# Two transformer blocks on one core: other start addresses for the split hidden activations of the six feed-forward layers

## The chip, the cores and the metric

The kernel runs on one core of one Trainium2 chip. The metric is the device time of one launch in microseconds: the median of three runs of the kernel before is 1599.71 us (1599.46 to 1599.98).

## The reference

Two blocks run one after the other on 256 tokens of 1024 features, in float32. Each block surrounds its mixers (three kinds of attention merged by gates in the first; a short convolution and a sparse attention in the second) with SwiGLU feed-forward layers, six of them in all:

```python
D_MODEL = 1024
SEQ = 256
D_FF = 2816

def swiglu(x, w_gate, w_up, w_down):
    return (jax.nn.silu(x @ w_gate) * (x @ w_up)) @ w_down

x = layer_norm(alpha * x + 0.5 * swiglu(x, w_gate[0], w_up[0], w_down[0]), ...)
x = layer_norm(alpha * x + hybrid_mixer(x, ...), ...)
x = layer_norm(alpha * x + 0.5 * swiglu(x, w_gate[1], w_up[1], w_down[1]), ...)
```

The change concerns only the last product of `swiglu`, hidden (256 x 2816) times `w_down` (2816 x 1024).

## The kernel before

Every float32 product is made of three products of the type fp32r. Both operands are split into a rounded high part and the rest as a low part, and high*high, low*high and high*low are added up in PSUM. ACT writes the high part (a copy that rounds), DVE the low part (original minus high part). Weights stream from HBM in slabs of 2048 elements per partition through six slots of `raw`; ACT makes `w_hi` and DVE `w_lo` from each (L729, L1160). Low parts overwrite `raw`.

`PHASES` (L49) gives the order of ten phases: six feed-forward layers (`FFN`), the mixer, the convolution, the keys and values, and the sparse attention. A feed-forward layer uses 33 slabs. The first 22 make the hidden activations, 256 features at a time (`tile(j)`, j = 0 to 10). In most tiles the weights are the stationary operand (`features`, L2089 and L2094), so that the result already has its features on partitions; the first two or three tiles have tokens as stationary operand and are turned by a transpose (`hidden`, L2077). Either way ACT and DVE leave the hidden activations as `hT_hi` and `hT_lo`, 22 chunks of 128 features by 256 tokens, in element order `[P, FC, S]` with `FC` = 22 and `S` = 256: ACT at L1096 and L1115, DVE at L1775 and L1794. In between, `silu` and `h` hold the two halves of a tile.

The last 11 slabs are the down product, done by `project` (L1870s). Here the split hidden activations are the stationary operand, 128 features by 128 tokens per weight load, and 512 columns of a weight slab are the moving operand. Per slab, `part` issues eight matmuls high*high, eight low*high, and eight high*low, in this order:

```python
for c, toks, at, o in each:
    nc.tensor.matmul(o, lhs_hi[:, 2 * d + c, toks], hi[:, c, at], ...)      # L1878
for i, (c, toks, at, o) in enumerate(each):
    nc.tensor.matmul(o, lhs_lo[:, 2 * d + c, toks], hi[:, c, at], ...)      # L1883
for c, toks, at, o in each:
    ins = nc.tensor.matmul(o, lhs_hi[:, 2 * d + c, toks], lo[:, c, at], ...)  # L1887
```

That is 24 matmuls for each of 11 slabs, 264 a layer and 1584 in the six layers. Each has a weight load (LDWEIGHTS) of its own.

Memory is laid out by the order of allocation. `layer_memory` frees what it allocates at once, so that the groups of tensors of different phases lie over each other. With `h_pad` (32 elements, 128 bytes), which nothing reads or writes, `hT_hi` starts at byte 179840 of each partition and `hT_lo` at 202368; both are 128 bytes past a multiple of 512. `silu` and `h` follow at 224896 and 226944, also at 128. `xT`, all slots of `w_hi` and of `w_lo`, and the similar operands `oT_hi` and `yT_hi` with their low parts start at 128 past such a multiple too, and 128 fp32r columns are 512 bytes, so every load of 128 fp32r columns in this kernel starts there. Two other groups of fp32r loads do not. In the compression of keys and values (L2383, L2384, L2389) a load has 80 columns and starts at `windows_of(xc_hi)[:, kv, c, part:part + 80]`, with `XC_ROW` = 96 elements from chunk to chunk and `xc_hi` at 0 past a multiple of 512: for `part` 0 the starts are multiples of 128 bytes, for `part` 1 each is 4 bytes further. In the gate product of the sparse attention (L1845, L1846, L1847) a load of `wg_hi` or `wg_lo` has 48 columns and starts at a multiple of 64 bytes.

Of the kernel before, what the change touches and what calls it, by code (L numbers as in the profile page):

```python
# [5 lines left out]
F32 = mybir.dt.float32  # L6
F32R = mybir.dt.float32r
# [5 lines left out]
P = 128  # L13
D = 1024
KC = D // P
S = 256
# [3 lines left out]
FC = FF // P  # L20
# [37 lines left out]
def two_block_kernel(nc, t, out):  # L58
# [5 lines left out]
    with ExitStack() as ctx:  # L64
# [7 lines left out]
        def layer_memory(tensors):  # L72
            with ExitStack() as own:
                return [own.enter_context(nc.sbuf_tensor(n, s, d)) for n, s, d in tensors]
# [32 lines left out]
        MERGED_FIRST = [(0, 0, bank[6]), (1, 0, bank[7]), (0, 1, bank[0]), (1, 1, bank[1])]  # L107

        qk, v_mix, _, oT_hi, oT_lo, gates, b_gate, prob, probT, far, tmp, o_norm = layer_memory([
            ("qk", [P, 6 * BC, S], F32),  # L110
            ("v_mix", [P, NT, 3 * BW], F32),
            ("o_pad", [P, 96], F32),
            ("oT_hi", [P, BC, S], F32R), ("oT_lo", [P, BC, S], F32R),
            ("gates", [P, NT, D], F32), ("b_gate", [P, 3, D], F32),
            ("prob", [P, 2, BW], F32),
            ("probT", [P, 2, BW], F32),
            ("far", [P, BW], F32),
# [35 lines left out]
        q_n = sel_pT[:].rearrange("p a b c -> p (a b c)")[:, 0:NT * D].rearrange("p (t n c) -> p t n c", t=NT, n=2)  # L153
        gate_rows = sel_add[0:3 * NQ, 0:S]
        cmp_l = sel_add[:].rearrange("p (t h n) -> p t h n", t=NT, h=NQ)
        _, hT_hi, hT_lo, silu, h = layer_memory([
            ("h_pad", [P, 32], F32),
            ("hT_hi", [P, FC, S], F32R), ("hT_lo", [P, FC, S], F32R),
            ("silu", [P, NT, 256], F32), ("h", [P, NT, 256], F32)])
        conv_v, conv_a, conv_c, conv_y, _, yT_hi, yT_lo, conv_b = layer_memory([  # L160
            ("conv_v", [P, KC, S + 2], F32), ("conv_a", [P, KC, S], F32), ("conv_c", [P, 2, 512], F32),
            ("conv_y", [P, 2, 512], F32), ("y_pad", [P, 16], F32), ("yT_hi", [P, KC, S], F32R), ("yT_lo", [P, KC, S], F32R),
# [148 lines left out]
        def tail(n):  # L311
            return TAIL + 1 if has_ln(n) and has_rms(n) else TAIL
# [19 lines left out]
        def token_tiles(n):  # L332
            return 3 if n == 0 or behind_kv(n) else 2
# [4 lines left out]
        def hidden_bank(n, j):  # L338
            return bank[4 + j % 2] if token_tiles(n) == 3 else bank[6 + j]
# [382 lines left out]
        def _(act):  # L722
# [10 lines left out]
            def split_to(k):  # L733

                while highs[0] <= k:
                    split(highs[0])
                    highs[0] += 1
# [25 lines left out]
            def boundary(n):  # L763
                split_to(first_slab[n + 1] + 5 - tail(n))
                if n < last:
                    for tt in range(NT):
                        norm(n, [tt])
                        if tt == 1:
                            split_to(first_slab[n + 1] + 3)
                        evacuate_input(inputs_before(n + 1), TOKENS_FIRST[2 * tt:2 * tt + 2], 2 * tt)  # L770
                        if tt == 0 and has_ln(n):
                            split_to(first_slab[n + 1] + 3)
# [22 lines left out]
            for n, kind in enumerate(phases):  # L795
# [293 lines left out]
                    boundary(n)  # L1089
                if kind == FFN:  # L1090
                    f = ffn_number[n]

                    def hidden(j):

                        act.wait_ge(hT_psum, token_before[n] + j + 1)
                        nc.scalar.activation(hT_hi[:, 2 * j:2 * j + 2, :],  # L1096
                                             hidden_bank(n, j)[:].rearrange("p (c m) -> p c m", c=2),
                                             ACT.Copy).then_inc(hT_high, 1)

                    def feature_tile(j):  # L1100

                        before, done = FT * f + j, joined_before[n] + j - token_tiles(n)
                        split_to(s0 + 2 * j + LEAD)
                        act.wait_ge(slab_used, s0 + 2 * j + 2)
                        act.wait_ge(h_ready, 2 * before)
                        for fb in range(2):
                            nc.scalar.activation(silu[:, fb, :], FEATURES[j % 2][fb][:, S:2 * S], ACT.Copy).then_inc(low_half, 1)  # L1107
                        act.wait_ge(hT_ready, before)
                        for fb in range(2):
                            nc.scalar.activation(h[:, fb, :], FEATURES[j % 2][2 + fb][:, S:2 * S], ACT.Copy).then_inc(low_half, 1)  # L1110
                        split_to(s0 + 2 * j + 1 + LEAD)
                        act.wait_ge(gate_joined, done + 1)
                        nc.scalar.activation(silu[:], silu[:], ACT.Silu).then_inc(silu_ready, 2)  # L1113
                        act.wait_ge(h_ready, 2 * before + 2)
                        nc.scalar.activation(hT_hi[:, 2 * j:2 * j + 2, :], h[:], ACT.Copy).then_inc(hT_high, 1)  # L1115

                    def tile(j):
                        if 0 < j <= token_tiles(n):
                            hidden(j - 1)
                        if j >= token_tiles(n):  # L1120
                            feature_tile(j)
                            return
                        split_to(s0 + 2 * j + LEAD)
                        act.wait_ge(slab_used, s0 + 2 * j + 2)
                        for tt in range(NT):
                            if j > 0:
                                act.wait_ge(h_ready, 2 * FT * f + 2 * j - 1 + tt)
                            nc.scalar.activation(silu[:, tt, :], bank[2 * (j % 2) + tt][:, 0:256],
                                                 ACT.Silu).then_inc(silu_ready, 1)
                        split_to(s0 + 2 * j + 1 + LEAD)  # L1130

                    for j in range(3):
                        tile(j)
                    if n == 0:
                        act.wait_ge(lam_dots, 1)
                        nc.scalar.activation(lam_col[:, 2:4], lam_col[:, 0:2], ACT.Exp).then_inc(lam_exp, 1)
                    for j in range(3, FT):
                        tile(j)
                    for d in range(FC // 2):
                        if d < FC // 2 - tail(n):  # L1140
                            split_to(s0 + 2 * FT + d + LEAD)
                    boundary(n)

        @block.vector
        def _(dve):
# [145 lines left out]
            for n, kind in enumerate(phases):  # L1291
# [477 lines left out]
                    boundary(n, 1.0, s0 + 8)  # L1769
                if kind == FFN:  # L1770
                    f = ffn_number[n]

                    def hidden(j):
                        dve.wait_ge(hT_high, FT * f + j + 1)
                        nc.vector.tensor_tensor(hT_lo[:, 2 * j:2 * j + 2, :],  # L1775
                                                hidden_bank(n, j)[:].rearrange("p (c m) -> p c m", c=2),
                                                hT_hi[:, 2 * j:2 * j + 2, :].bitcast(F32),
                                                ALU.subtract).then_inc(hT_ready, 1)
# [63 lines left out]
        def _(pe):  # L1842
# [216 lines left out]
            for n, kind in enumerate(phases):  # L2059
                s0 = first_slab[n]  # L2060
                if kind == FFN:
                    f = ffn_number[n]

                    def gate_up(j, kh, tiles=range(NT)):
                        ins = token_slab(s0 + 2 * j + kh, kh, 512, slice(0, 512), lambda tt: bank[2 * (j % 2) + tt][:], tiles=tiles)
                        if NT - 1 in tiles:
                            ins.then_inc(slab_used, 1)
# [291 lines left out]
                if kind == KV:  # L2359
# [12 lines left out]
                    for kv in range(2):  # L2372

                        pe.wait_ge(xc_ready, 1 + 4 * (kv + 1))
                        for part in range(2):
# [4 lines left out]
                            for c in range(8):  # L2380
                                chunk = 8 * part + c
                                at = slice(part, part + CMP_ROWS)
# [3 lines left out]
                            for c in range(8):  # L2386
                                chunk = 8 * part + c
                                at = slice(part, part + CMP_ROWS)
# [7 lines left out]
                if kind == NSA:  # L2396
# [141 lines left out]
                    for tt in range(NT):  # L2538
                        unit_gone(tt)
                        for g in range(GROUPS):  # L2540
                            p = cmp_p[:, tt, PER_GROUP * g:PER_GROUP * (g + 1), :].rearrange("p r n -> p (r n)")
# [50 lines left out]
```

## Time and profile before

| | |
|---|---|
| median of three runs | 1599.71 us |
| span of the profiled execution, first to last instruction | 1597.9 us |
| that execution's span to the median of the runs | 1.8 us less |
| TensorE busy (matmul) | 1591.1 us |
| VectorE busy | 1031.5 us |
| ScalarE busy | 801.4 us |
| moved by DMA | 291.21 MB |
| mean granted clock of TensorE | 1.000 |

The device time of a run holds the span and some 1.8 us around it. Busy time of matmuls overlaps, since they are pipelined: one of 512 columns shows about 390 ns while the next starts after some 227 ns. What a matmul costs in a stream is therefore read from the distance between starts, and the timeline, which merges equal instructions that follow each other, gives it: the start of one row to the start of the next, divided by the count.

### The profile page before, as it was taken

The page shows a single profiled execution, that of the slowest core. Times are in us where ns is not written, and L with a number is a line of the kernel's source. Part 1 is how long each engine was busy: PE and PEld are TensorE (multiplying, and loading weights), DVE is VectorE, ACT ScalarE, POOL GpSimd, SP SyncE. Part 2 cuts the span into 40 slices and gives each one's busy share as a digit, 9 for nine tenths or more (in the row PEclk, how much of TensorE's full clock was granted, in tenths as well). Part 3 has the DMA queues.
Part 4 walks back from the last instruction along what each step waited for, and adds up shares of the span by engine and source line. Part 5 has one row for each costly group of instructions (what it writes and reads, how often), then busy time and mean ns, then how long its engine had stood idle before and what let it go on. Part 6 is the DMA issues. An engine that isn't in the chain of part 4 may idle for free.

```text
span 1597.9 us, 21193 instructions
## 1 busy us (share of the span) xinstructions
PE 1591.1 (100%) x8788; PEld 1369.5 (86%) x8788; DVE 1031.5 (65%) x1228; ACT 801.4 (50%) x1092; POOL 35.5 (2%) x53
## 2 busy tenths in 40 slices
PE   9999999999999999999999999999999999999999
PEld 7888898878888888888899888889888888988887
DVE  6665656798766647665557666557766557766662
ACT  5555254775455525554344555446555436545550
POOL 0000000000000000000000000001000011000000
PEclk9999999999999999999999999999999999999999
DMA  9565574445567546665465655558565551056551
GB/s 308 187 218 184 171 260 154 141 139 181 170 196 231 199 163 199 194 200 186 157 224 176 194 185 203 197 171 254 175 189 199 187 198 56 28 174 192 187 186 77
DMA packets 226591, 291.21 MB, mean 182 GB/s; under 512 B 10628, under 2 KB 203840, under 8 KB 226368
## 3 DMA queue, kind: packets, MB, share of 16 engines
q1 hardware_dynamic: 226224, 289.61, 55.2%
q8 instruction: 69, 1.13, 0.3%
q10 hardware_dynamic: 272, 0.26, 0.0%
q14 instruction: 26, 0.21, 0.0%
HBM read 288.78 MB, written 1.05 MB: 181 GB/s over the span
## 4 chain that ended last, share of the span: by engine, by line
PE 95%; DVE 3%; ACT 1%; POOL 0%; issue 0%; DVEq 0%
PE bank L2089 24%; PE bank L2094 12%; PE bank L1878 9%; PE bank L1883 9%; PE bank L1887 9%; PE bank L1966 6%; PE bank L1958 6%; PE bank L1953 6%; PE bank L1927 2%; PE bank L1934 2%; PE bank L1929 2%; PE bank L2496 1%; PE bank L1854 1%; DVE w_lo L1160 1%; PE bank L2460 1%; PE bank L2471 1%
## 5 line engine op out<-in xcount | busy, mean ns | idle before, releaser
L1160 DVE TENSOR_TENSOR w_lo<-raw,w_hi 128x2048 fp32r<-128x2048 f32 (+1 forms) x267 | 599.3, 2269 | 166.8 <-ACT w_hi L729 164.5
L729 ACT ACTIVATE w_hi<-raw 128x2048 fp32r<-128x2048 f32 (+1 forms) x266 | 504.9, 1905 | 169.0 <-DMA raw<-in_ffn_w_down_dram 93.4
L2089 PE MATMUL bank<-xT,w_hi 128*128 128x512 f32 x1664 | 397.3, 391 | 0.0
L2089 PEld LDWEIGHTS bank<-xT,w_hi 128*128 128x128 f32 x1664 | 306.2, 188 | 59.5
L2094 PEld LDWEIGHTS bank<-xT,w_lo 128*128 128x128 f32 x1664 | 213.3, 191 | 8.1
L2094 PE MATMUL bank<-xT,w_lo 128*128 128x256 f32 x1664 | 215.9, 283 | 0.0
L1107 ACT ACTIVATE silu<-bank 128x256 f32<-128x256 f32 x104 | 34.2, 381 | 215.9 <-PE bank L2094 215.9
L1883 PE MATMUL bank<-w_hi,hT_lo 128*128 128x512 f32 x528 | 134.9, 390 | 0.0
L1878 PE MATMUL bank<-w_hi,hT_hi 128*128 128x512 f32 x528 | 133.8, 389 | 0.0
L1887 PE MATMUL bank<-w_lo,hT_hi 128*128 128x512 f32 x528 | 133.7, 389 | 0.0
L1953 PE MATMUL bank<-w_hi,xT 128*128 128x512 f32 (+2 forms) x448 | 117.6, 391 | 0.0
L1887 PEld LDWEIGHTS bank<-w_lo,hT_hi 128*128 128x128 f32 x528 | 99.1, 188 | 20.6
L1878 PEld LDWEIGHTS bank<-w_hi,hT_hi 128*128 128x128 f32 x528 | 98.7, 188 | 20.3
L1883 PEld LDWEIGHTS bank<-w_hi,hT_lo 128*128 128x128 f32 x528 | 98.8, 188 | 20.2
L1966 PE MATMUL bank<-w_lo,xT 128*128 128x512 f32 (+2 forms) x456 | 115.3, 384 | 0.1
L1958 PE MATMUL bank<-w_hi,xT 128*128 128x512 f32 (+2 forms) x448 | 114.4, 384 | 0.0
L1966 PEld LDWEIGHTS bank<-w_lo,xT 128*128 128x128 f32 x456 | 84.4, 188 | 17.1 <-DVE w_lo L1160 0.5
L1792 DVE TENSOR_TENSOR h<-silu,h 128x512 f32<-128x512 f32 x52 | 36.0, 692 | 96.3 <-ACT silu L1113 96.3
L1958 PEld LDWEIGHTS bank<-w_hi,xT 128*128 128x128 f32 x448 | 82.9, 188 | 16.7 <-issue 0.2
L1953 PEld LDWEIGHTS bank<-w_hi,xT 128*128 128x128 f32 x448 | 80.4, 188 | 15.5 <-DVE xT L1174 0.7
L1787 DVE TENSOR_TENSOR silu<-bank,silu 128x256 f32<-128x256 f32 x104 | 39.2, 419 | 71.0 <-ACT silu L1107 71.0
L743 ACT ACTIVATE xT<-bank 128x512 fp32r<-128x512 f32 x48 | 26.5, 598 | 97.6 <-PE bank L1854 97.5
(294 smaller groups left out, 1572.4 us busy)
## 6 DMA issues: line engine op xcount, KB each, us to landing
raw<-in_ffn_w_gate_up_dram SPq DMA_DIRECT2D x176, 512.0 KB, 4.8
raw<-in_ffn_w_down_dram SPq DMA_DIRECT2D x132, 512.0 KB, 4.1
raw<-in_w_in_dram SPq DMA_DIRECT2D x44, 512.0 KB, 4.9
raw<-in_ffn_w_gate_dram SPq DMA_DIRECT2D x42, 512.0 KB, 4.0
raw<-in_ffn_w_up_dram SPq DMA_DIRECT2D x42, 512.0 KB, 5.0
raw<-in_conv_w_in_dram SPq DMA_DIRECT2D x24, 512.0 KB, 4.6
raw<-in_kv_w_dram SPq DMA_DIRECT2D x12, 512.0 KB, 4.4
raw<-in_w_out_dram SPq DMA_DIRECT2D x8, 512.0 KB, 3.9
```

Source lines behind the costliest of these rows:

```text
L729: nc.scalar.activation(w_hi[:, slot, 0:width], raw[:, slot, 0:width], ACT.Copy).then_inc(high_ready, 1)
L1160: nc.vector.tensor_tensor(w_lo[:, slot, 0:width], raw[:, slot, 0:width], w_hi[:, slot, 0:width].bitcast(F32), ALU.subtract).then_inc(low_r ...
L1787: ins = nc.vector.tensor_tensor(part[:, fb % 2, :], FEATURES[j % 2][fb][:, 0:S], part[:, fb % 2, :], ALU.add)
L1792: nc.vector.tensor_tensor(h[:], silu[:], h[:], ALU.mult).then_inc(h_ready, 2)
L1878: nc.tensor.matmul(o, lhs_hi[:, 2 * d + c, toks], hi[:, c, at], start=d == 0 and c == 0, stop=False, skip_group_check=True)
L1883: nc.tensor.matmul(o, lhs_lo[:, 2 * d + c, toks], hi[:, c, at], start=False, stop=False, skip_group_check=True)
L1887: ins = nc.tensor.matmul(o, lhs_hi[:, 2 * d + c, toks], lo[:, c, at], start=False, stop=d == slabs - 1 and c == 1, skip_group_check=True)
L1953: nc.tensor.matmul(dst(tt), xT_hi[:, 4 * kh + c, toks], hi[:, c, at], start=kh == 0 and c == 0 and not (shared and tt), stop=False, skip_g ...
L1958: nc.tensor.matmul(dst(tt), xT_lo[:, 4 * kh + c, toks], hi[:, c, at], start=False, stop=False, skip_group_check=True)
L1966: ins = nc.tensor.matmul(dst(tt), xT_hi[:, 4 * kh + c, tt * P:(tt + 1) * P], lo[:, c, at], start=False, stop=kh == 1 and c == 3, skip_grou ...
L2089: nc.tensor.matmul(o[:], hi[:, c, at], x, start=kh == 0 and c == 0, stop=False, skip_group_check=True)
L2094: ins = nc.tensor.matmul(o[:, 0:S], lo[:, c, at], xT_hi[:, 4 * kh + c, :], start=False, stop=kh == 1 and c == 3, skip_group_check=True)
```

## The change

```diff
-        _, hT_hi, hT_lo, silu, h = layer_memory([
-            ("h_pad", [P, 32], F32),
-            ("hT_hi", [P, FC, S], F32R), ("hT_lo", [P, FC, S], F32R),
+        hT, silu, h = layer_memory([
+            ("hT", [P, 2 * FC * S + 112], F32R),
             ("silu", [P, NT, 256], F32), ("h", [P, NT, 256], F32)])
+        HT_STARTS = [(0, 64), (4, 36), (8, 96), (16, 48), (1, 33), (32, 40)]
+
+        def hT_of(f):
+            return [hT[:, at:at + FC * S].rearrange("p (c m) -> p c m", c=FC)
+                    for at in (HT_STARTS[f][0], FC * S + HT_STARTS[f][1])]
+
...
                 if kind == FFN:
                     f = ffn_number[n]
+                    hT_hi, hT_lo = hT_of(f)
```

The last line is added in the programs of ScalarE, VectorE and TensorE. The two operands now lie in one tensor `hT` that starts at byte 179712, a multiple of 512, and each feed-forward layer f places them by its own pair of `HT_STARTS`, in elements of 4 bytes. No instruction is added, removed or moved on any engine; only addresses differ. Where they start, in bytes past a multiple of 512:

| layer f | high part | low part |
|---|---|---|
| before, all six | 128 | 128 |
| 0 | 0 | 256 |
| 1 | 16 | 144 |
| 2 | 32 | 384 |
| 3 | 64 | 192 |
| 4 | 4 | 132 |
| 5 | 128 | 160 |

`silu` and `h` move by 320 bytes, to 448 past a multiple of 512. Of the 264 matmuls of a layer 176 load the high part and 88 the low part.

## Rows read from the trace of the kernel before

**Rows 1.** The page: the span, and busy time of each engine.
```profile
span 1597.9 us, 21193 instructions
...
PE 1591.1 (100%) x8788; PEld 1369.5 (86%) x8788; DVE 1031.5 (65%) x1228; ACT 801.4 (50%) x1092; POOL 35.5 (2%) x53
```

**Rows 2.** The page: the chain that ended last, by engine.
```profile
PE 95%; DVE 3%; ACT 1%; POOL 0%; issue 0%; DVEq 0%
```

**Rows 3.** Granted clock of the core over the span.
```profile
core 0: 1597.9 us, clock 1.000
```

**Rows 4.** The page's groups for the down product: busy, mean ns, idle before.
```profile
L1883 PE MATMUL bank<-w_hi,hT_lo 128*128 128x512 f32 x528 | 134.9, 390 | 0.0
L1878 PE MATMUL bank<-w_hi,hT_hi 128*128 128x512 f32 x528 | 133.8, 389 | 0.0
L1887 PE MATMUL bank<-w_lo,hT_hi 128*128 128x512 f32 x528 | 133.7, 389 | 0.0
...
L1878 PEld LDWEIGHTS bank<-w_hi,hT_hi 128*128 128x128 f32 x528 | 98.7, 188 | 20.3
```

**Rows 5.** Timeline of PE, down product of layer 0: start us, us, what.
```profile
137.11 1.98 PE L1878 MATMUL bank<-w_hi,hT_hi 128*128 128x512 f32 x8
...
169.75 0.62 PE L1878 MATMUL bank<-w_hi,hT_hi 128*128 128x512 f32 x2
```

**Rows 6.** Timeline of PE, down product of layer 5.
```profile
1540.17 1.98 PE L1878 MATMUL bank<-w_hi,hT_hi 128*128 128x512 f32 x8
...
1551.05 1.98 PE L1878 MATMUL bank<-w_hi,hT_hi 128*128 128x512 f32 x8
```

**Rows 7.** Groups of weight loads of 80 and 48 columns, shapes kept apart.
```profile
L2383 PEld LDWEIGHTS bank<-w_hi,xc_hi 128*80 128x80 f32 x32 | 4.7, 148 | 0.0
...
L1846 PEld LDWEIGHTS bank<-xT,wg_hi 128*48 128x48 f32 x8 | 1.0, 121 | 0.0
```

**Rows 8.** Timeline of PE, compression, first starts on multiples of 128 bytes.
```profile
1098.66 0.28 PE L2384 MATMUL bank<-w_hi,xc_lo 128*80 128x256 f32 x1
...
1099.91 1.07 PE L2389 MATMUL bank<-w_lo,xc_hi 128*80 128x256 f32 x8
...
1105.20 0.28 PE L2383 MATMUL bank<-w_hi,xc_hi 128*80 128x256 f32 x1
...
1106.33 1.08 PE L2389 MATMUL bank<-w_lo,xc_hi 128*80 128x256 f32 x8
```

**Rows 9.** The same, starts 4 bytes past them.
```profile
1100.82 0.28 PE L2383 MATMUL bank<-w_hi,xc_hi 128*80 128x256 f32 x1
...
1102.69 1.11 PE L2389 MATMUL bank<-w_lo,xc_hi 128*80 128x256 f32 x8
...
1107.62 0.28 PE L2383 MATMUL bank<-w_hi,xc_hi 128*80 128x256 f32 x1
...
1109.26 1.11 PE L2389 MATMUL bank<-w_lo,xc_hi 128*80 128x256 f32 x8
```

**Rows 10.** Timeline of PE, gate product: loads of 48 columns.
```profile
1326.51 0.28 PE L1846 MATMUL bank<-xT,wg_hi 128*48 128x256 f32 x1
...
1327.64 0.28 PE L1847 MATMUL bank<-xT,wg_hi 128*48 128x256 f32 x1
```

**Rows 11.** Timeline of PE: 256 moving columns with loads of 128 columns.
```profile
129.73 2.08 PE L2094 MATMUL bank<-xT,w_lo 128*128 128x256 f32 x16
131.64 1.55 PE L1878 MATMUL bank<-w_hi,hT_hi 128*128 128x512 f32 x6
```

**Rows 12.** Instructions that write hT_hi and hT_lo: min/median/max ns, first and last start.
```profile
L1115 ACT ACTIVATE hT_hi<-h x52: 631/632/633, 59.7 to 1539.3; 128x512 fp32r<-128x512 f32 x52
L1794 DVE TENSOR_TENSOR hT_lo<-h,hT_hi x52: 691/693/694, 60.4 to 1540.0; 128x512 fp32r<-128x512 f32 x52
```

**Rows 13.** Waits of ACT, the longest: total us, times, longest us.
```profile
ACT silu L1107 <- PE bank L2094: 215.9, 52, 4.3
```

More of the change, by code:

```diff
@@ L1771, in _ @@
                     f = ffn_number[n]
+                    hT_hi, hT_lo = hT_of(f)
                     def hidden(j):
@@ L2062, in _ @@
                     f = ffn_number[n]
+                    hT_hi, hT_lo = hT_of(f)
                     def gate_up(j, kh, tiles=range(NT)):
```

## The prediction

> **What bounds the kernel now.** I read the page's totals first. TensorE runs matmuls for 1591.1 us of a span of 1597.9 us [rows 1]; the next engine, DVE, is busy for 1031.5 us. The chain of work that ended last agrees: 95% of it is PE [rows 2]. So the time is the number of matmuls times the distance between their starts, and a change of addresses matters if it changes that distance, or if it makes another engine so slow that PE waits. The clock was granted in full for the whole span [rows 3], which is the 2.4 GHz level: 512 moving columns take 213.3 ns and 256 take 106.7 ns.
>
> Then I read the distance. In the timeline of layer 0 the stretch from 137.11 to 169.75 us holds 144 matmuls (18 rows of 8) [rows 5]: 32.64 / 144 = 226.7 ns each. Layer 5 gives 10.88 us for 48, again 226.7 [rows 6]. The columns alone would take 213.3, so 13.3 ns per matmul are something else. It isn't waiting: the three groups of the down product have 0.0 us of idle time before them [rows 4]. Nor is it the length of the load. A load of 128 columns takes 188 ns [rows 4], less than the 226.7 between starts, and where the moving operand has 256 columns the same kind of load is followed by a matmul every 119.4 ns (1.91 us for 16) [rows 11]. So beside 512 moving columns a load could be some 100 ns slower and PE would not see it. The question is only whether the 13.3 ns depend on where the load starts.
>
> **What the trace says of start addresses.** All loads of 128 fp32r columns start 128 bytes past a multiple of 512, so no row shows another offset at full width. The nearest rows are the narrower loads. With 80 columns and 256 moving ones, starts at 0, 128, 256 and 384 past a multiple of 512 give 1.25 us for 11 matmuls and 1.13 us for 10 [rows 8]: 2.38 / 21 = 113.3 ns. These four offsets can't be told apart. With starts 4 bytes further on, the same code gives 1.87 us for 16 and 1.64 us for 14 [rows 9]: 3.51 / 30 = 117.0 ns. The two kinds alternate within 11 us, and their loads both last 148 ns [rows 7], so 3.7 ns per matmul go with the 4 bytes. With 48 columns, in starts that step through all multiples of 64, 1.13 us for 10 is 113.0 ns [rows 10]. What I take from this: on multiples of 64 bytes the offset costs nothing, 4 bytes off them it costs 3.7 ns, and starts that are multiples of 16 but not of 64 are not shown.
>
> Two statements of the Trainium skill bear on this. The page "TensorE: Matmul & The Clock Gate" says, in its step-by-step section, that the next tile's weight load has a read port of its own and takes nothing from the running matmul. By that rule no offset could matter and the time stays 1599.7. The pair 113.3 and 117.0 ns speaks against it: the load lasts as long, and the matmuls still come later. The page "SBUF — State Buffer" gives in its specifications 16-byte lines, and says that each crossing to a new line costs something. By that rule only starts off multiples of 16 bytes would add a line, which is layer 4 alone; my reading of the sum would then be 1600.7.
>
> **The sum.** The 1584 matmuls of the down products divide by start:
> - 176 don't move (layer 5, high part): 0.
> - 616 go to another multiple of 64 bytes (layer 0 both parts, 264; layer 2 low, 88; layer 3 both, 264). Nearest rows: 113.3 and 113.0 ns at all such starts. I take 0.
> - 264 are 4 bytes off (layer 4, starts 4 and 132). Lower end 3.7 ns as with 80 columns, upper end 3.7 x 128/80 = 5.9 ns if it grows with the columns. The lower end is the measured one, and I take it: 264 x 3.7 = 0.98 us. The upper end gives 1.56.
> - 528 start on a multiple of 16 that is not one of 64 (layer 1 both, 264; layer 2 high at 32, 176; layer 5 low at 160, 88). Bounds: 0 as on the 64-byte grid, and 5.9 ns as above. Nothing says which neighbour they resemble, so I take half of the measured price, 1.85 ns: 0.98 us. The ends are 0 and 3.1 us.
>
> The rest of the edit costs nothing on the path. ACT and DVE write the hidden activations to the new starts, in 632 and 693 ns, and touch `silu` and `h` at 448 instead of 128. No row shows such writes at another offset. But ACT waits for PE 52 times for 215.9 us in all, some 4.2 us per feature tile [rows 13], and DVE has 566 us of slack in the span [rows 1]. Both would have to get slower by microseconds in each tile before PE noticed. If that cover were gone, each 0.1 us on the pair [rows 12] would cost at most 66 x 0.2 = 13 us, but a doubling is not in sight. The down product itself needs tile 10 only for its last slab, which comes after at least eight and a half slabs' worth of matmuls (8.5 x 24 x 226.7 ns = 46 us), so even a late write has room. The 56 transposes that load `h` and the warm-up matmuls at the start go from one multiple of 64 to another: 0, on the reading above. Loads and queues are untouched, and so are instruction counts.
>
> Sum: 0.98 + 0.98 = 1.96 us. On the profiled execution this is 1597.9 + 2.0 = 1599.9 us of span; the median of the runs stands 1.8 us above the span, so 1599.7 + 2.0 = **1601.7 us**. With the ends (0.98 below, 1.56 + 3.1 = 4.7 above) this case spans 1600.7 to 1604.4. About 0.2% (3.2 us) is what a measurement of this kernel can tell from no change, so most of the case counts as no change.
>
> **Rivals.**
> - *Full-width loads collide with the stream unless both start alike* (slower). Now stationary and moving operand both start 128 past a multiple of 512, and both are read at the same time. A load of 128 columns costs 12.7 ns beyond the 106.7 of its columns (119.4), one of 80 or 48 columns only 6.6 (113.3), and the narrow ones are all that rows 8 and 10 speak for. If the wide load pays again what it already pays over a narrow one, 119.4 - 113.3 = 6.1 ns, whenever its start differs from that of the stream, it is 1408 x 6.1 = 8.6 us: 1608.3. If it pays its full 13.3 ns twice, 18.7 us: 1618.4. It decides for slower from 3.2 / 1408 = 2.3 ns per matmul on. For it: the difference between widths is real and unexplained. Against it: the 80-column loads cross multiples of 512 too, with a moving operand that starts at 128, and show no offset dependence.
> - *The common start is itself the collision* (faster). Then those 6.1 ns vanish wherever the starts differ: 1599.7 - 8.6 = 1591.1. If it were the whole 13.3 it would be 1581.0. Against it: with 80 columns, the start at 128 is not slower than those at 0, 256 and 384.
> - *Nothing happens*: the 3.7 ns belong to the odd windows of the compression, or are hidden under 512 moving columns, where they were measured under 256. Time 1599.7.
>
> **Chances.** Forecast 0.42, collision 0.32, gain 0.13, nothing 0.13. The collision gets much, since it rests on the width that the trace does not show at any other start. No change within 0.2% holds the whole of nothing and 0.34 of the forecast: 0.47. Slower is the collision and the upper 0.08 of the forecast: 0.40. Faster is 0.13. The range takes in nothing and the forecast (0.55) and the collision up to 8.7 ns per matmul, 12.3 us, which I put at 0.25 of its 0.32; that is 1598.5 to 1612.0, with the lower end 1.2 us under no change, and leaves out 0.2.
>
> **What would show it.** Each layer has its own pair of starts, so the timeline of the changed kernel gives a table by itself: microseconds per row of eight matmuls at L1878 and L1887 for the high start, at L1883 for the low one. Before, each is 1.81. The forecast wants 1.81 in layers 0 and 3, 1.84 at all three lines in layer 4, and 1.81 to 1.84 in layer 1, at L1878 and L1887 in layer 2, and at L1883 in layer 5. The collision wants 1.86 or more everywhere but at L1878 and L1887 of layer 5, and the gain 1.77 or less there. If layers 0 and 3 move at all, the step "multiples of 64 cost nothing" is wrong; if layer 4 does not move, the price from the 80-column loads is. Loads should keep 188 ns and the groups 0.0 us of idle time; an idle time that shows up before L1883 would mean that a writer became late, which I have put at nothing.

## The result and the profile after

The changed kernel takes 1605.86 us (1605.78 to 1606.07, 4 runs), the kernel before 1599.83 us in the same session (1599.46 to 1599.98, 4 runs). The ratio is 1.0038, with a 95% interval of 1.0026 to 1.0051: 6.0 us slower, and clear of noise.

The page of the changed kernel, lines that answer to [rows 1] and [rows 4]: span, busy time of the engines, and the groups of the down product, whose three lines are now L1885, L1890 (low part) and L1894.

```profile
span 1604.0 us, 21193 instructions
...
PE 1597.5 (100%) x8788; PEld 1369.7 (85%) x8788; DVE 1031.8 (64%) x1228; ACT 801.4 (50%) x1092; POOL 35.6 (2%) x53
...
L1890 PE MATMUL bank<-w_hi,hT 128*128 128x512 f32 x528 | 137.4, 394 | 0.0
L1894 PE MATMUL bank<-w_lo,hT 128*128 128x512 f32 x528 | 135.7, 393 | 0.0
L1885 PE MATMUL bank<-w_hi,hT 128*128 128x512 f32 x528 | 135.3, 392 | 0.0
L1894 PEld LDWEIGHTS bank<-w_lo,hT 128*128 128x128 f32 x528 | 99.2, 188 | 22.9
```

PE's busy time grew by 6.4 us; DVE and ACT hold what they held. The three groups of the down product now have 408.4 us where they held 402.4 [rows 4], which is the 6.0 us. They still have 0.0 us of idle time before them, the loads still last 188 ns, and the clock is granted in full. So nobody waits for anybody: the matmuls simply start further apart. Which ones do can be read from the timeline of PE in layer 4 (high part at 4, low at 132), to set against [rows 5, 6]:

```profile
1248.05 1.98 PE L1885 MATMUL bank<-w_hi,hT 128*128 128x512 f32 x8
1249.88 2.02 PE L1890 MATMUL bank<-w_hi,hT 128*128 128x512 f32 x8
1251.74 2.02 PE L1894 MATMUL bank<-w_lo,hT 128*128 128x512 f32 x8
1253.60 1.98 PE L1885 MATMUL bank<-w_hi,hT 128*128 128x512 f32 x8
```

Start to start, eight matmuls take 1.83, 1.86 and 1.86 us, where all took 1.81. The surprise is in the first and third row: both load the same high part from the same addresses, and both streams start at 128, yet they take 1.83 and 1.86 us. And in layer 0 and layer 1:

```profile
163.35 2.02 PE L1894 MATMUL bank<-w_lo,hT 128*128 128x512 f32 x8
165.21 2.02 PE L1885 MATMUL bank<-w_hi,hT 128*128 128x512 f32 x8
...
544.46 1.98 PE L1894 MATMUL bank<-w_lo,hT 128*128 128x512 f32 x8
546.27 1.98 PE L1885 MATMUL bank<-w_hi,hT 128*128 128x512 f32 x8
```

Layer 0 needs 1.86 us a row, layer 1 still 1.81. From the first to the last start of a down product each layer took 60.53 us before (layer 5 59.64, as no next layer's transposes stand within it). The differences after, from the same two starts:

| layer | high/low start | more than before, us |
|---|---|---|
| 0 | 0 / 256 | 1.45 |
| 1 | 16 / 144 | 0.00 |
| 2 | 32 / 384 | 1.52 |
| 3 | 64 / 192 | 1.12 |
| 4 | 4 / 132 | 1.26 |
| 5 | 128 / 160 | 0.70 |

They add up to 6.05 us, the whole of the difference. In a slow layer the distances are not merely longer, they go round in a cycle. In layer 0 the starts are about 232, 228, 230, 232, 241, 232 and 231 ns apart, over and over. In a fast one they are 226 or 227, now and then 225 or 228. In the kernel before, each layer's down product begins with five longer ones (233, 236, 228, 233 and 231 in layer 0) and is at 226 or 227 from there on.

### The profile page after: what moved, and what is told of

Read it like the earlier page. It is cut to its first block, busy times and chain, and to the rows that moved or that the text cites. A ratio compares the mean times of both kernels' runs of the same rounds, so it can differ in the third digit from the quotient of the medians.

```text
span 1604.0 us, 21193 instructions
## 1 busy us (share of the span) xinstructions
PE 1597.5 (100%) x8788; PEld 1369.7 (85%) x8788; DVE 1031.8 (64%) x1228; ACT 801.4 (50%) x1092; POOL 35.6 (2%) x53
## 4 chain that ended last, share of the span: by engine, by line
PE 95%; DVE 3%; ACT 1%; POOL 0%; issue 0%; DVEq 0%
PE bank L2097 24%; PE bank L2102 12%; PE bank L1890 9%; PE bank L1885 9%; PE bank L1894 9%; PE bank L1973 6%; PE bank L1965 6%; PE bank L1960 6%; PE bank L1934 2%; PE bank L1941 2%; PE bank L1936 2%; PE bank L2504 1%; PE bank L1861 1%; DVE w_lo L1166 1%; PE bank L2468 1%; PE bank L2479 1%
## 5 line engine op out<-in xcount | busy, mean ns | idle before, releaser
L2097 PE MATMUL bank<-xT,w_hi 128*128 128x512 f32 x1664 | 397.4, 391 | 0.0
L2097 PEld LDWEIGHTS bank<-xT,w_hi 128*128 128x128 f32 x1664 | 306.1, 188 | 59.7
L1890 PE MATMUL bank<-w_hi,hT 128*128 128x512 f32 x528 | 137.4, 394 | 0.0
L1894 PE MATMUL bank<-w_lo,hT 128*128 128x512 f32 x528 | 135.7, 393 | 0.0
L1885 PE MATMUL bank<-w_hi,hT 128*128 128x512 f32 x528 | 135.3, 392 | 0.0
L1894 PEld LDWEIGHTS bank<-w_lo,hT 128*128 128x128 f32 x528 | 99.2, 188 | 22.9
L1890 PEld LDWEIGHTS bank<-w_hi,hT 128*128 128x128 f32 x528 | 98.8, 188 | 22.4
L1885 PEld LDWEIGHTS bank<-w_hi,hT 128*128 128x128 f32 x528 | 98.8, 188 | 21.5
```

The lines of the kernel that those rows point to most:

```text
L2097: nc.tensor.matmul(o[:], hi[:, c, at], x, start=kh == 0 and c == 0, stop=False, skip_group_check=True)
```

## The experiments

All edits are to `HT_STARTS` of the changed kernel, or to the allocations of the kernel before. Starts are in bytes past a multiple of 512, and the stream of weight columns starts at 128 unless said otherwise.

### Layer 0's pair, and layer 1's, in all layers

```diff
-        HT_STARTS = [(0, 64), (4, 36), (8, 96), (16, 48), (1, 33), (32, 40)]
+        HT_STARTS = [(0, 64)] * 6
```

> The pair of layer 0 (high at 0, low at 256 past a multiple of 512) in all six layers. Theory A (the price belongs to the start of the load, layer by layer): each layer gets layer 0's 61.98 us in place of 60.53, so 6 x 1.45 = 8.7 us over before, 1608.5. Rival (the rise belongs to changing the starts from layer to layer, or to silu and h at 448, not to the start itself): 1599.8 to 1606.

Measured 1608.44 us, ratio 1.0054 (1.0039 to 1.0069), 8.6 us over before. Every layer takes 1.44 to 1.47 us more, as theory A wanted.

```diff
+        HT_STARTS = [(4, 36)] * 6
```

> The pair of layer 1 (16 and 144) in all six layers. Theory A: 226.7 ns per matmul in every layer, as before, so 1599.8. Rival (what matters is silu and h at 448, or the layout with one tensor): slower than before by more than 1 us.

Measured 1599.78 us, ratio 1.0 (0.9991 to 1.001). This has the one tensor `hT`, and `silu` and `h` at 448, and costs nothing. So the price is neither the layout, nor the writes of ACT and DVE, nor the change from layer to layer; it goes with the starts, pair by pair.

### Is it the load's start, or its distance from the stream's?

```diff
+        sb("front_pad", [P, 32])
         raw, = layer_memory([("raw", [P, SLOTS, SLAB], F32)])
```

> From the kernel before: 32 unused elements ahead of everything, so that all operands, stationary and moving, start at 256 instead of 128 past a multiple of 512, and all differences between them stay. Relative theory (what counts is the load's start against the start of the stream): 1599.8, 226.7 ns in all full-width groups. Absolute theory (a start at 256 is slow as such): the nearly 6,900 full-width fp32r loads all pay; at 5.5 ns each about 38 us more, 1637, and L2094 too.

Measured 1599.78 us, ratio 0.9999 (0.999 to 1.0009), as the relative theory wanted. Loads and streams at 256 are as fast as at 128, although loads at 0 and 256 over a stream at 128 had been slow.

```diff
+        sb("front_pad", [P, 32])
...
-            ("h_pad", [P, 32], F32),
```

> The same 32 elements in front, and h_pad taken out, so that the hidden activations stay at 128 while the streams move to 256: the difference is 128 below, as in layer 0's high part. Relative theory: the six down products run at about 232 ns in place of 226.7, 1584 x 5.5 ns = 8.7 us more than before (1608.5), all else as before. Absolute theory: down products fast at 226.7, all other full-width groups slow.

Measured 1608.23 us, ratio 1.0052 (1.0037 to 1.0067), again as the relative theory wanted. Here the hidden activations lie where they always lay, and only the stream moved. The groups of this run against those of the run with 0 and 256 everywhere (first fence this one, second that one):

```profile
L1883 PE MATMUL bank<-w_hi,hT_lo 128*128 128x512 f32 x528 | 137.8, 395 | 0.0
L1887 PE MATMUL bank<-w_lo,hT_hi 128*128 128x512 f32 x528 | 136.7, 395 | 0.0
L1878 PE MATMUL bank<-w_hi,hT_hi 128*128 128x512 f32 x528 | 136.6, 394 | 0.0
```

```profile
L1890 PE MATMUL bank<-w_hi,hT 128*128 128x512 f32 x528 | 137.8, 395 | 0.0
L1894 PE MATMUL bank<-w_lo,hT 128*128 128x512 f32 x528 | 136.7, 395 | 0.0
L1885 PE MATMUL bank<-w_hi,hT 128*128 128x512 f32 x528 | 136.6, 394 | 0.0
```

They agree to 0.1 us. Moving the stream by 128 does what moving the load by 128 does, and moving both does nothing. An absolute start has no price at these steps; the two reads have one together.

### Is it only the down products?

In both kernels that follow `hT` stays, and `xT` moves against all weight slabs.

```diff
+        stats = sb("stats", [P, 64])
         xT = sb("xT", [P, KC, 2, S], F32R)
...
-        stats = sb("stats", [P, 64])
```

> The kernel before with xT 256 bytes further (stats allocated ahead of it), and all other operands where they were. The relative theory holds for any pair of load and stream: the some 3,130 matmuls with 512 moving columns that pair xT with a weight slab pay as a difference of 256 did (5.6 ns): 17.5 us. For the some 2,580 with 256 moving columns (L2094, L1927, L1929, L1934) no row shows a price; 0 to 5.6 ns, up to 14.4 us. So 1617 to 1632, and the down products stay at 226.7. Rival (the price belongs to the down products alone): 1599.8.

Measured 1599.83 us in one run, beside 1599.51. The expectation missed by 17 us: a difference of 256 is no difference. In the runs with 0 and 256 both parts had been 128 off, one below and one above.

```diff
+        head_max = sb("head_max", [P, 2, 4])
+        head_sum = sb("head_sum", [P, 2, 4])
+        cols = sb("cols", [P, 80])
         xT = sb("xT", [P, KC, 2, S], F32R)
...
-        head_max = sb("head_max", [P, 2, 4])
-        head_sum = sb("head_sum", [P, 2, 4])
...
-        cols = sb("cols", [P, 80])
```

> After a shift of xT by 256 changed nothing: the difference counts modulo 256, so xT moved by 384 (cols, head_max and head_sum allocated ahead of it; nothing else that is a fp32r operand moves) is 128 off against every weight slab. Theory (any pair of load and stream pays): L2089 and the other some 1,470 matmuls that pair xT with 512 moving columns go from 227 to about 232 ns, 3,130 x 5.6 = 17.5 us; L2094 and the other 256-column ones 0 to 5.6 ns. So 1617 to 1632, down products unchanged. Rival (it belongs to the down products' own pair of operands): 1599.8.

Measured 1611.01 us, ratio 1.0071 (1.0054 to 1.0088): 11.4 us slower, so the effect is not the down products' own, but less than the 17 expected. Groups of the kernel before, and then of this run, shapes apart:

```profile
L2089 PE MATMUL bank<-xT,w_hi 128*128 128x512 f32 x1664 | 397.3, 391 | 0.0
L2094 PE MATMUL bank<-xT,w_lo 128*128 128x256 f32 x1664 | 215.9, 283 | 0.0
...
L1966 PE MATMUL bank<-w_lo,xT 128*128 128x512 f32 x424 | 109.6, 390 | 0.1
```

```profile
L2089 PE MATMUL bank<-xT,w_hi 128*128 128x512 f32 x1664 | 404.6, 395 | 0.0
L2094 PE MATMUL bank<-xT,w_lo 128*128 128x256 f32 x1664 | 214.4, 281 | 0.0
...
L1966 PE MATMUL bank<-w_lo,xT 128*128 128x512 f32 x424 | 111.8, 395 | 0.0
```

L2089 pays 7.3 us, which is 4.4 ns for each of 1664 and not 5.6. L2094, with 256 moving columns, gains 1.5 us: the same distance that slows a stream of 512 columns speeds up one of 256.

### Which starts, and does the neighbour matter?

Four kernels put a new pair in each layer. Their edits, high and low start in elements of 4 bytes, with the expectations in the same order below:

```diff
+ sweep_a  HT_STARTS = [(1, 36), (2, 36), (12, 36), (4, 33), (32, 36), (20, 36)]
+ sweep_b  HT_STARTS = [(4, 6), (4, 24), (4, 28), (4, 52), (4, 68), (4, 100)]
+ sweep_c  HT_STARTS = [(3, 36), (5, 36), (6, 36), (24, 36), (28, 36), (34, 36)]
+ sweep_d  HT_STARTS = [(1, 1), (28, 28), (96, 96), (33, 33), (60, 60), (112, 112)]
```

> Starts by layer, high/low, in bytes past a multiple of 512, the stream at 128: 4/144, 8/144, 48/144, 16/132, 128/144, 80/144. Theory R1 (what counts is the difference load minus stream; it is free where it is 0, or 16 past a multiple of 128 as for 16 and 144): low parts at 144 and the high ones at 16 and 128 at 226.7 ns, those at 4, 8, 48 and 80 slow by 3 to 7 ns, low at 132 slow. That makes layer 4 60.5 us, layer 3 about 61.0 and layers 0, 1, 2 and 5 up to 61.5. Rival R2 (once the stream has fallen out of step it stays out, whatever follows): in layers 0, 1, 2 and 5 the low part at 144 is slow as well, and they cost 61.8 to 62.1.

> High part at 16 in all layers, low at 24, 96, 112, 208, 272, 400. R1: low is free at 272 and 400 (16 past a multiple of 128), slow at 24, 96, 112 and 208; so layers 4 and 5 as before, layers 0 to 3 at 60.9 to 61.1 us (88 loads x 4 to 7 ns). Rival R3 (free only at differences within 16 of 0, and 16 itself by chance): 272 and 400 slow too. In no layer is a matmul expected under 226.7 ns; if one of these starts is faster, a kernel that uses it everywhere would beat both.

> Low part at 144 in all layers, high at 12, 20, 24, 96, 112, 136. R1: all six high starts slow, low free; each layer up to 61.5 us. If 12, 20 or 24 are free, the free places are a band around 16 and not a point. R2: low at 144 slow as well wherever the high part is.

> High and low part at the same start in each layer: 4, 112, 384, 132, 240, 448; each layer then shows one difference by itself, without a neighbour that upsets it. Theory H (each start has a fast and a slow rhythm, and which one runs is handed on from the matmuls before): 4 and 384 at 226.7 (60.53 us), 132 and 448 slow (61.6 to 62.2), and 112 slow at about 229 although the low part at 112 was free behind a high part at 16; 240, which is 112 but for 128, is not predicted. Rival (each start has one price of its own): 112 free, at 60.53 us. None is expected under 226.7 ns.

One run each: 1606.02, 1602.78 and 1607.39 us beside 1599.51, and 1605.09 beside 1599.66. What each layer took more than before, in us, with the mean distance from the matmul before to each of the low part's (L1890) in ns, both from the starts in the trace:

| high/low | more | low part | high/low | more | low part |
|---|---|---|---|---|---|
| 4/144 | 0.0 | 226.7 | 12/144 | 1.4 | 229.9 |
| 8/144 | 1.6 | 232.8 | 20/144 | 1.7 | 233.7 |
| 48/144 | 1.2 | 233.0 | 24/144 | 1.2 | 231.8 |
| 16/132 | 1.7 | 232.8 | 96/144 | 1.1 | 226.7 |
| 128/144 | 0.0 | 226.7 | 112/144 | 0.9 | 233.2 |
| 80/144 | 1.6 | 233.3 | 136/144 | 1.3 | 233.3 |
| 16/24 | 1.1 | 231.4 | 4/4 | 0.0 | 226.7 |
| 16/96 | 0.6 | 233.3 | 112/112 | 0.4 | 228.3 |
| 16/112 | 0.0 | 226.6 | 384/384 | 0.0 | 226.7 |
| 16/208 | 1.4 | 232.3 | 132/132 | 1.4 | 232.5 |
| 16/272 | 0.0 | 226.6 | 240/240 | 1.7 | 233.3 |
| 16/400 | 0.0 | 226.6 | 448/448 | 1.7 | 233.3 |

Theory R1, one price per start, fails: the same low part at 144 runs at 226.7 ns behind a high part at 4, 16 (the run above), 96 or 128, and at 231.8 to 233.7 behind 8, 20, 24, 48, 80, 112 or 136. R2, once out of step always out, fails too: behind 96 (itself slow) 144 is fast again at once, and behind 12 it comes back after three matmuls. R3 fails as well, since 272 and 400 are free behind 16. Sweep D put the theory that replaced them to the test, and it held: 112, free behind a high part at 16, was forecast slow by itself. The timelines of PE, first behind 16 (sweep B), then alone (sweep D):

```profile
731.78 1.98 PE L1885 MATMUL bank<-w_hi,hT 128*128 128x512 f32 x8
733.59 1.98 PE L1890 MATMUL bank<-w_hi,hT 128*128 128x512 f32 x8
735.40 1.97 PE L1894 MATMUL bank<-w_lo,hT 128*128 128x512 f32 x8
737.22 1.98 PE L1885 MATMUL bank<-w_hi,hT 128*128 128x512 f32 x8
```

```profile
544.85 1.99 PE L1885 MATMUL bank<-w_hi,hT 128*128 128x512 f32 x8
546.68 1.99 PE L1890 MATMUL bank<-w_hi,hT 128*128 128x512 f32 x8
548.51 1.99 PE L1894 MATMUL bank<-w_lo,hT 128*128 128x512 f32 x8
```

The rows of L1890 load from 112: 1.81 us to the next row in the one, 1.83 in the other. What differs is the matmuls around them. So a start has more than one rhythm, and the one it runs in is handed on by the matmuls before. Not all hand-overs are lasting. 384, a difference of 256 and so like 128, began its layer with distances of 234, 236, 228, 232 and 231 ns and was at 227 from there on, as 128 does in the kernel before. But eight matmuls are not always enough for it: in layer 2 of the changed kernel the low part starts at 384 too, behind a high part at 32, and its matmuls come 231.2 ns apart in the mean. Nor do only equal starts come back: 16 behind 96 is at 226 or 227 from its first matmul on.

No start of the 24 pairs gave less than 226.6 ns.

### A version faster than both?

L2094 had gained in one run, so the low weights, its loads, were put elsewhere, at a distance that had been free where they are the stream.

```diff
-        w_lo = sb("w_lo", [P, SLOTS, SLAB], F32R)
+        w_lo = sb("w_lo", [P, SLOTS * SLAB + 64], F32R)
+        w_lo = w_lo[:, LOW_AT:LOW_AT + SLOTS * SLAB].rearrange("p (s n) -> p s n", s=SLOTS)
```

`raw` has the same shape and offset; `LOW_AT` is 28, then 60.

> A try to be faster than both: in the run with xT off by 384 the 1,968 matmuls of 256 moving columns with low weights (L2094, L1934) came 0.8 and 1.2 ns closer. Here only raw and w_lo lie elsewhere, 112 further modulo 256 (at 240); w_hi and everything behind it move by 256, which is nothing. Where w_lo is the stream under xT, hT, yT or oT the difference is -112, as for 16 under 128 (free); where w_lo is the load (L2094, L1934) it is +112, not seen yet with 256 columns. If that gives the same 0.8 to 1.2 ns: 1.6 to 2 us less, 1597.7 to 1598.2. If not, L2094 pays up to 3.7 ns (as the 80-column loads off by 4): up to 7 us more. L1887 and L1966 stay at 226.7.

Measured 1608.96 us, ratio 1.0057 (1.0045 to 1.007): 9.1 us slower, more than either branch of the expectation allowed. Its groups of the down product, which held 133.8, 133.7 and 134.9 us before [rows 4]:

```profile
L1881 PE MATMUL bank<-w_hi,hT_hi 128*128 128x512 f32 x528 | 136.2, 394 | 0.0
L1890 PE MATMUL bank<-w_lo,hT_hi 128*128 128x512 f32 x528 | 135.7, 392 | 0.0
L1886 PE MATMUL bank<-w_hi,hT_lo 128*128 128x512 f32 x528 | 135.7, 391 | 0.0
```

The loads from `w_lo` gained nothing (216.2 us against 215.9). The stream from `w_lo` (L1890), 144 below its load and so 112 above it modulo 256, was not free. And L1881, whose own load and stream start alike, grew most: its eight matmuls behind each slow row are followed by the next start after 229, 235, 233, 236, 224, 231, 236 and 228 ns, the first two of L1886 after 233 and 230, and only then the distances are 226 or 227. That is the hand-over again, and it lasts for ten matmuls with equal starts.

> The same with w_lo at 112: under xT and hT the difference is +16 (as for 144 over 128, free), and as a load it is -16 against xT. 1597.7 to 1598.2 if L2094 and L1934 gain 0.8 to 1.2 ns there, up to 1607 if they pay as loads off the grid do; L1887 and L1966 at 226.7 either way.

Measured 1602.27 us, ratio 1.0016 (1.0007 to 1.0025). Groups of this second run:

```profile
L2097 PE MATMUL bank<-xT,w_lo 128*128 128x256 f32 x1664 | 211.9, 279 | 0.0
L1890 PE MATMUL bank<-w_lo,hT_hi 128*128 128x512 f32 x528 | 137.2, 396 | 0.0
...
L1969 PE MATMUL bank<-w_lo,xT 128*128 128x512 f32 x424 | 112.2, 396 | 0.0
```

The matmuls of L2097 gained 4.0 us (215.9 before), twice what was hoped. The groups in which `w_lo` is the stream lost it again and more: 3.5 and 2.6 us in these two. That was not expected, and it bounds the theory. A load at 144 over a stream at 128 is free, and one at 384 over a stream at 368 is 16 off as well and runs at 233 ns. The run before says the same: a load at 16 over a stream at 128 is free, one at 384 over a stream at 240 has the same difference modulo 256 and is not. So the difference alone is shown to decide only while both starts move by 128. No kernel of the study beats the kernel before.

## Why the prediction was right, and where its steps were not

The direction and the range held: slower by 6.0 us, inside 1598.5 to 1612.0. The likeliest time did not: 1601.7 us stood for 2.0 us, and the case's own range ended at 1604.4. By the chances, too, no change within 0.2% stood first with 0.47, and slower, which came, had 0.40. So the sum did not carry the prediction: the range held because it gave room to the first rival, and what happened is nearest to that rival.

- *The bound.* PE sets the time, and only the distance between starts could matter. Right: the three groups hold all of the 6.0 us.
- *The 616 at multiples of 64 are free.* This step failed, and it is most of the miss. Layer 0 took 1.45 us (264 at 5.5 ns), layer 3 took 1.12. The narrow loads, from which the zero came, stood over 256 moving columns and not 512: over a stream that starts at 128 too they are all alike at 0, 128, 256 and 384 (113.3 ns), while full-width loads over 512 columns are fast at 128 and 384 and slow at 0 and 256. The rows differ in two things, the width of the load and the number of moving columns, and no run takes them apart: no narrow load stands over 512 columns, and full-width loads over 256 columns moved by 0.9 ns the other way (L2094 in the run with `xT` 384 further).
- *The 528 at multiples of 16 at half the price.* The sum of 0.98 us was too small, and the sorting was wrong: layer 1 (16 and 144) was free, and layer 5's low part and layer 2 paid, 0.70 and 1.52 us with layer 2's low part in it.
- *The 264 of layer 4 at 3.7 ns.* 0.98 us forecast, 1.26 measured. But it came unevenly: L1885 took some 1.8 ns, L1890 and L1894 6.3 and 6.7 (means of 228.5, 233.0 and 233.4 ns between starts). And being 4 bytes off is not what costs: in sweep A and D a high part at 4, and both parts at 4, took 0.0 us more. Of the layer's two starts only 132 is slow by itself. The price from the 80-column loads got near by luck.
- *Everything else costs nothing.* Right, and shown by the run with 16 and 144 in all layers: `silu` and `h` at 448, one tensor, other places for the writes, 1599.78 us.
- *The rival "full-width loads collide with the stream unless both start alike".* Its price of 6.1 ns was close: most slow starts cost 5.5 to 6.6 ns. Nothing in the runs ties that price to the difference between load widths from which it was taken, so its size is luck as far as is known. Its 1408 payers were too many. Layer 1 and part of layer 4 do not pay, and layer 3 pays 4.2 ns a matmul. "Unless both start alike" is too narrow, since 4, 16, 272 and 400 over 128 are free as well, and differences count modulo 256 where multiples of 128 were tried.
- *The independent read port of the Trainium skill* ("TensorE: Matmul & The Clock Gate", the step-by-step section). By it nothing could happen. The runs speak against it: with unchanged loads of 188 ns, the stream alone moved by 128 bytes made 1584 matmuls 8.4 us slower.
- *The 16-byte lines* ("SBUF — State Buffer", specifications). By them only layer 4 would have paid. Layer 0, at 0 and 256, paid more than layer 4.

What stays open is the machinery beneath: why the distances of a slow start go round in cycles, and why one rhythm is kept and another lost. The table says which pairs are slow, and the runs say that load and stream make the price together. That a shared read path lets one of them through at a time is a guess that none of these runs shows.

## What to carry to other kernels

Where PE is the bound and fp32r matmuls follow each other without gaps, the addresses of the operands are part of the kernel's speed: start the stationary and the moving operand at the same offset modulo 256 bytes, and pad for it, in all streams that follow each other, since a slow neighbour slows equal starts as well for up to ten matmuls. The runs show this for offsets of 128 and 256, with equal starts nowhere slower than another pair at 512 moving columns. Other start addresses cost 0.2 to 0.7% in these runs, with no wait and no longer load to show for it; the cost is seen only in the distance between starts, or in a group's busy time at the same count. And rows on narrow loads over 256 moving columns did not bound full-width loads over 512.

## What was not expected of the hardware

- The same kind of matmul, with the same two starts modulo 512 bytes, has two speeds, by what ran before it: 226.7 and about 233 ns for the load at 144; 226.7 and 228.3 for the one at 112.
- With 512 moving columns a distance of 128 bytes costs 4.4 to 5.6 ns per matmul; with 256 it gains 0.9 (L2094, 215.9 to 214.4 us). Low weights as loads at 368 over a stream at 384 gain 2.4 ns (215.9 to 211.9 us). A layout that gives L2094 this place and keeps `w_lo` at 128 where it is the stream wasn't tried; by these rows an estimate of its gain is 4 us.
- Moving `xT` by 256 bytes changed neither the 397.3 us of L2089 nor the 215.9 us of L2094 by 0.1 us.
